# Hybrid encoder step on one core: the first branch's two early gates as a fourth Strassen pair, and two selection rounds moved

## What is computed

```python
h = rmsnorm(x, norm_mix)
(a_b, a_c, a_x, qb, kb, vb, qc, kc, vc, qi, ki, wi, g_a, g_b, g_c) = jnp.split(h @ w_in, SPLIT_POINTS, axis=-1)
y_conv, new_conv_a = causal_dwconv(a_c * a_x, conv_a_buf, conv_a)      # width 512
br_a = (a_b * y_conv) @ w_a_out                                        # 512 -> 1024
# br_b: attention in a window of 128; br_c: attention on the 256 keys that an indexer scores highest
merged = jax.nn.sigmoid(g_a) * br_a + jax.nn.sigmoid(g_b) * br_b + jax.nn.sigmoid(g_c) * br_c
x = x + merged @ w_out
```

## Time and profile before

| | |
|---|---|
| median of 3 runs | 1754.98 us (1754.83 to 1756.56) |
| profiled execution | 1755.11 us, span 1753.3 us |
| granted TensorE clock | 0.997 of full speed |
| busy, share of span | PE 98%, DVE 76%, ACT 43%, POOL 32% |
| DMA | 146.41 MB, mean 84 GB/s |

### The profile page before, as it was taken

How to read it: one execution, slowest core, us unless ns; L and a number is a source line. 1 busy time by engine, 2 the same in 40 slices (tenths; PEclk the granted TensorE clock), 3 DMA queues, 4 the chain that set the end, 5 groups by cost and what they waited for, 6 DMA issues and landing times.

```text
span 1753.3 us, 32227 instructions
## 1 busy us (share of the span) xinstructions
PE 1719.3 (98%) x12251; PEld 1679.9 (96%) x12251; DVE 1337.9 (76%) x2190; ACT 752.6 (43%) x1323; POOL 567.4 (32%) x457
## 2 busy tenths in 40 slices
PE   6999999999999999999999999999999999999998
PEld 6999999999999999888899999999999999999998
DVE  6689899868799996788759989766666665875765
ACT  5344323368721234767744563333333333422334
POOL 2211722267745431000021102655555554121030
PEclk9999999999999999999999999999999999999999
DMA  4101111111143414422324111222222222533212
GB/s 157 49 25 43 48 39 54 49 29 37 47 146 120 144 40 148 154 85 85 109 79 154 49 49 50 93 79 84 76 74 82 77 86 92 185 116 98 75 37 99
DMA packets 179189, 146.41 MB, mean 84 GB/s; under 512 B 10140, under 2 KB 149676, under 8 KB 179052
## 3 DMA queue, kind: packets, MB, share of 16 engines
q1 hardware_dynamic: 178076, 142.54, 26.2%
q0 software_dynamic: 976, 2.00, 0.5%
HBM read 118.22 MB, written 26.28 MB: 82 GB/s over the span
## 4 chain that ended last, share of the span: by engine, by line
PE 91%; DVE 4%; ACT 2%; issue 1%; POOL 1%; DMA 0%; SPq 0%; DVEq 0%; ACTq 0%; POOLq 0%
PE ps L1600 29%; PE ps L2079 23%; PE ps L2152 7%; PE ps L2138 7%; PE ps L1795 4%; PE ps L1775 4%; PE ps L1612 4%; PE ps L1712 4%; PE ps L2009 3%; PE ps L1921 3%; PE ps L1869 1%; PE ps L1630 1%; PE ps L1876 1%; ACT probs L2535 0%; DMA x_rows<-in_x_prompt 0%
## 5 line engine op out<-in xcount | busy, mean ns | idle before, releaser
L1600 PE MATMUL ps<-h_hi,w_hi 128*128 128x352 f32 (+1 forms) x768 | 168.5, 328 | 0.0
L1600 PE MATMUL ps<-h_hi,w_lo 128*128 128x352 f32 (+1 forms) x768 | 165.6, 323 | 0.0
L1600 PE MATMUL ps<-h_lo,w_hi 128*128 128x352 f32 (+1 forms) x768 | 165.2, 323 | 0.0
L1287 POOL TENSOR_TENSOR w_lo<-w_raw,w_hi 128x512 fp32r<-128x512 f32 (+1 forms) x45 | 84.9, 1886 | 236.7 <-ACT w_hi L2240 236.6
L3169 DVE MAX8 top<-key_mask 128x8 f32<-128x896 f32 (+5 forms) x166 | 151.9, 917 | 8.9 <-DVE key_mask L3169 1.4
L3169 DVE MATCH_REPLACE8 key_mask<-top,key_mask 128x896 f32<-128x896 f32 (+5 forms) x166 | 149.4, 904 | 0.0
L2079 PE MATMUL ps<-mix_hi,quarter_hi 128*128 128x264 f32 x672 | 136.9, 285 | 0.2 <-ACT x_one L2240 0.2
L2079 PE MATMUL ps<-mix_hi,quarter_lo 128*128 128x264 f32 x672 | 136.5, 285 | 0.0
L2079 PE MATMUL ps<-mix_lo,quarter_hi 128*128 128x264 f32 x672 | 136.1, 284 | 0.0
L1600 PEld LDWEIGHTS ps<-h_hi,w_lo 128*128 128x128 f32 (+1 forms) x768 | 130.7, 186 | 0.5
L1600 PEld LDWEIGHTS ps<-h_hi,w_hi 128*128 128x128 f32 (+1 forms) x768 | 128.8, 187 | 2.6 <-issue 0.9
(11 more groups left out here) (455 smaller groups left out, 4930.3 us busy)
## 6 DMA issues: line engine op xcount, KB each, us to landing
w_raw<-in_w_in SPq DMA_DIRECT2D x54, 256.0 KB, 3.1
w_hi<-gate_highs SPq DMA_DIRECT2D x48, 256.0 KB, 2.8
w_lo<-gate_lows SPq DMA_DIRECT2D x48, 256.0 KB, 3.1
ffn_tiles<-t SPq DMA_DIRECT2D x44, 264.0 KB, 2.4
w_raw<-in_w_gate SPq DMA_DIRECT2D x44, 256.0 KB, 3.1
w_raw<-in_w_up SPq DMA_DIRECT2D x44, 256.0 KB, 3.1
w_raw_in_lo<-in_w_in SPq DMA_DIRECT2D x30, 256.0 KB, 3.0
w_raw<-in_w_down SPq DMA_DIRECT2D x32, 192.0 KB, 2.7
```

The source lines that it names most:

```text
L1287: nc.gpsimd.tensor_tensor(WLO[:, k, 0:tiles, :], raw[:, k, 0:tiles, :], WHI[:, k, 0:tiles, :].bitcast(F32), ALU.subtract).then_inc(lo_read ...
L1600: last = nc.tensor.matmul(PS[0:rows, NB * k + b, 0:e - a], w[:, k, t, 0:rows], x[:, t, a:e], start=m == 0 and w is WHI and x is hi, stop=m ...
```

## The change

- `A_PAIRS` gets a fourth pair, gate tiles 0 and 1 (`C_G`, `C_G + P`). The jobs J_GA and J_GA+9 go; J_GA is now the first `w_a_out` job, and all later jobs are numbered two lower.
- The fourth pair's two tiles are t0 and t1, like the third's. ACT's first copy of it therefore waits for `a_input(2)`, which now counts on `a_added`. Even pairs now use banks 0 and 1 where odd ones use 6 and 7 (before the other way round).
- `a_conv(3)` writes to `conv_gate3` in place of t1. `a_high(2)` comes after the fourth pair's second product, `a_high(3)` after its sixth. DVE does `a_input(2)` and `a_conv(3)` before `a_lower(2)`, and the fourth pair's adds before `a_lower(3)`.
- ACT takes `Tanh` of t0 and t1 in place. DVE multiplies tile 1 by its gate in step j=2 of the `w_a_out` loop, no longer after it.
- In `attention_jobs` of the window branch the rounds of `SEL[5]` become 1, 2, 3, 3, 1 for m=1 to m=5, from 3, 2, 3, 2, 0.

```diff
-J_B = J_GA + KT + 2
+J_B = J_GA + KT
...
-A_PAIRS = (..., (C_AC + 3 * P, C_AX + 3 * P))
-A_SLOTS = [n % 4 for n in range(NQ * len(A_PAIRS) - 1)] + [2]
+A_PAIRS = (..., (C_AC + 3 * P, C_AX + 3 * P),
+           (C_G, C_G + P))
+A_GATES = 2
+A_SLOTS = [n % 4 for n in range(NQ * len(A_PAIRS))]
...
-            x = 3 if p % 2 == 0 else 0
+            x = 0 if p % 2 == 0 else 3
...
-            return 3 * p + (p == 2)
+            return 3 * p + max(p - 1, 0)
...
-        A_TILES = [(B2, B3), (T1, T3), (T0, T1)]
-        A_RAW = (T1, T0, B2, T1)
+        A_TILES = [(B2, B3), (T1, T3), (T0, T1), (T0, T1)]
+        A_RAW = (T1, T0, B2, B3)
... (PE)
-            project(J_GA, 0, 0, H_HI, H_LO)
             pe.wait_ge(a_lo, CT + 1)
-            for n in range(J_GA + 1, J_B - 1):
+            for n in range(J_GA, J_B):
                 project(0, n // 2, n % 2, A_HI, A_LO, tiles=CT)
-            project(J_B - 2, 0, 1, H_HI, H_LO)
... (ACT)
-                    act.wait_ge(*((sums_ready, 2), (taken[1], evicted(J_GA - 1)), (a_lo, 3))[p])
+                    act.wait_ge(*((sums_ready, 2), (taken[1], evicted(J_GA - 1)), (a_lo, 3),
+                                  (a_added, landed(a_adds(3))))[p])
...
-                if n == NQ * len(A_PAIRS) - 3:
-                    split(J_GA, 0, 0)
                 if n == NQ * len(A_PAIRS) - 2:
+                    split(J_GA, 0, 0, tiles=CT)
+                if n == NQ * (len(A_PAIRS) - 1) + 1:
                     a_high(2)
-            following(J_GA, 0, 0, tiles=tiles_of(J_GA + 1))
-            a_high(CT - 1)
+                if n == NQ * len(A_PAIRS) - 2:
+                    a_high(3)
+            following(J_GA, 0, 0, tiles=CT)
... (DVE)
             a_add(2, Q_A12)
-            a_lower(2)
             a_input(2)
             a_conv(3, B3)
+            a_lower(2)
+            a_add(3, Q_S4)
+            a_add(3, Q_S3)
+            a_add(3, Q_A12)
             a_lower(3)
... (DVE)
             for j in range(KT):
-                n = J_GA + 1 + j
+                n = J_GA + j
                 done(0, n // 2, n % 2)
                 if j == 0:
-                    dve.wait_ge(taken[0], evicted(J_GA))
+                    dve.wait_ge(gate_out, 1)
                     V_.scalar_tensor_tensor(tile_at(MACC, j), tokens(T0[:, 0:TOK]), 1.0, group(n % 2), ALU.add,
                                             ALU.mult).then_inc(taken[n % 2], 1)
+                if j == 2:
+                    dve.wait_ge(gate_out, A_GATES)
+                    dve.wait_ge(taken[1], evicted(J_GA + 1))
+                    V_.scalar_tensor_tensor(tile_at(MACC, 1), tokens(T1[:, 0:TOK]), 1.0, tile_at(MACC, 1), ALU.add,
+                                            ALU.mult).then_inc(a_added, 1)
                 select((SEL[5], 2))
             select((SEL[5], 2), (SEL[3], 3))
-            dve.wait_ge(gate_out, 1)
-            V_.scalar_tensor_tensor(tile_at(MACC, 1), tokens(T0[:, 0:TOK]), 1.0, tile_at(MACC, 1), ALU.add,
-                                    ALU.mult).then_inc(taken[1], 1)
-            last_low = attention_jobs(J_B, 1, R_B_V, ((NT, TOPK_S // 8), (SEL[3], 2)), ((SEL[5], 3),),
-                                      ((SEL[5], 2), (SEL[3], 1)), ((SEL[5], 3),), ((SEL[5], 2),))
+            last_low = attention_jobs(J_B, 1, R_B_V, ((NT, TOPK_S // 8), (SEL[3], 2)), ((SEL[5], 1),),
+                                      ((SEL[5], 2), (SEL[3], 1)), ((SEL[5], 3),), ((SEL[5], 3),), ((SEL[5], 1),))
```

More of the change, by code:

```diff
@@ L102 @@
 DOWN_ORDER = (Q_A11, Q_S1, Q_S2, Q_S4, Q_S3, Q_A12, Q_A22)
[L107 to L108 removed]
+A_PAIRS = ((C_AB + 2 * P, C_AB + 3 * P), (C_AC + 2 * P, C_AX + 2 * P), (C_AC + 3 * P, C_AX + 3 * P),
+           (C_G, C_G + P))
+A_GATES = 2
+A_SLOTS = [n % 4 for n in range(NQ * len(A_PAIRS))]
 A_SUMS = (Q_S1, Q_S2, Q_S4, Q_S3)
@@ L222, in tiles_of @@
 def tiles_of(n):
-    branch = J_GA < n < J_B - 1 or J_GB <= n < J_C and (n - J_GB) % 2 == 1 or J_BC <= n < J_WO
+    branch = J_GA <= n < J_B or J_GB <= n < J_C and (n - J_GB) % 2 == 1 or J_BC <= n < J_WO
     return CT if branch else KT
@@ L1078, in attention_loads @@
                         load(k, plain(k, w_in[:, :, bass.ds(i * (2 * P) + (q + k * P), P)], to=WIN))
-            load_gate_a = lambda n, j: load(n % 2, plain(n % 2, columns(w_in, C_G + j * P)))
-            free_quarters(len(A_PAIRS), 0)
-            load_gate_a(J_GA, 0)
             for j in range(KT):
-                n = J_GA + 1 + j
-                if j == 0:
-                    free_quarters(len(A_PAIRS), 1)
+                n = J_GA + j
+                if j < 2:
+                    free_quarters(len(A_PAIRS), j)
                 else:
@@ L1089, in _ @@
                 load(n % 2, plain(n % 2, columns(w_a, j * P), CT))
-            free(J_B - 2, 0, 1)
-            load_gate_a(J_B - 1, 1)
             attention_loads(J_B, C_QB, (C_KB, C_VB))
@@ L1387, in sinks @@
                     nc.gpsimd.tensor_copy(columns, pair["negative"].unsqueeze(2)).then_inc(sink_in, 1)
-            pool.wait_ge(taken[1], evicted(J_B - 1))
+            pool.wait_ge(a_added, landed(a_adds(len(A_PAIRS) - 1) + 4))
             for y in range(3):
@@ L1401, in late_gate @@
                 w, p = q // NB, q % NB
-                pool.wait_ge(gate_out, 1 + q + 1)
+                pool.wait_ge(gate_out, A_GATES + q + 1)
                 acc = piece_at(MACC, LATE_GATES[w], p)
@@ L1725, in _ @@
                 if p == 0:
+                    pe.wait_ge(taken[0], evicted(J_GA - 2))
+                elif p == 1:
                     pe.wait_ge(rows_out, R_IDX_K + 3)
-                elif p == 1:
-                    pe.wait_ge(taken[0], evicted(J_GA - 2))
                 else:
@@ L1771, in late_gates @@
                     if q >= 2:
-                        pe.wait_ge(gate_out, 1 + q - 1)
+                        pe.wait_ge(gate_out, A_GATES + q - 1)
                     for t in range(KT):
@@ L1976, in _ @@
             attend_window(WINDOW)
-            pe.wait_ge(gate_out, 1 + len(LATE_GATES) * NB)
+            pe.wait_ge(gate_out, A_GATES + len(LATE_GATES) * NB)
             gates(J_GB, O_HI, O_LO, o_lo, NT + 1)
@@ L2412, in _ @@
                     a_weight_high(n + 4)
-                if n == NQ * len(A_PAIRS) - 3:
-                    split(J_GA, 0, 0)
                 if n == NQ * len(A_PAIRS) - 2:
+                    split(J_GA, 0, 0, tiles=CT)
+                if n == NQ * (len(A_PAIRS) - 1) + 1:
                     a_high(2)
-            following(J_GA, 0, 0, tiles=tiles_of(J_GA + 1))
-            a_high(CT - 1)
[L2419 to L2423, removed]
+                if n == NQ * len(A_PAIRS) - 2:
+                    a_high(3)
+            following(J_GA, 0, 0, tiles=CT)
+            act.wait_ge(a_added, landed(a_adds(len(A_PAIRS) - 1) + 3))
+            act.wait_ge(a_copied, landed(5 * len(A_PAIRS)))
+            for gate in A_TILES[-1]:
+                nc.scalar.activation(gate[:, 0:TOK], gate[:, 0:TOK], ACT.Tanh, scale=0.5).then_inc(gate_out, 1)
+            for n in range(J_GA, J_B):
+                if n > J_GA:
+                    following(0, n // 2, n % 2, tiles=tiles_of(n + 1))
                     done(0, n // 2, n % 2)
[L2425 to L2428, removed]
+                    copy(tile_at(MACC, n - J_GA), group(n % 2)).then_inc(taken[n % 2], 1)
             def late_gate(q):
@@ L2472, in attention_jobs @@
                 if n0 == J_B:
+                    act.wait_ge(a_added, landed(a_adds(len(A_PAIRS) - 1) + 4))
                     act.wait_ge(stored[0], 32)
@@ L3298, in a_input @@
                 last = V_.tensor_tensor(U[:, SEQ + 4:TOK + 4], first[:, SEQ:TOK], second[:, SEQ:TOK], ALU.mult)
[L3299 to L3304, removed]
+                last.then_inc(a_added, 1)
+                dve.wait_ge(a_added, landed(a_adds(p + 1)))
             def a_add(p, q):
```

2 lines of the change are left out of this document (1 added, 1 removed).

## The result

The changed kernel takes **1758.58 us** (median of 22 runs, 1757.18 to 1759.75) against 1755.77 of the kernel before beside it (22 runs, 1754.6 to 1758.32): ratio 1.0016, interval 1.001 to 1.0021. It is 2.8 us slower. That is within the 0.2% which the prediction counted as no change, but above its figure of 1755.7 and outside its range, which ended at 1757.4. The forecast was built on 1754.98, the median of three runs; beside the changed kernel the median of 22 is 1755.77. So of the 2.9 us between forecast and measurement 0.8 are the base, and 2.1 are the change: +0.7 forecast, +2.8 measured. The profiled execution took 1759.71 us.

A forecast was written before the change was run, and what follows sets the result against it. PE was taken as the bound, busy 1719.3 of 1753.3 us. Terms -2.5 + 0.5 + 0.3 + 2.35 gave +0.7 on the 1754.98 us median, so 1755.7 us, range 1753.2 to 1757.4.

The forecast's parts named there:

- PE's work, -2.5: Fourth pair's 168 matmuls (20.8 us) replace two gates' 144 (23.3 us), so PE issues 2.5 us less.
- the 0.6 us of slack: In the fourth pair, ACT's first copy, waiting for `a_input(2)`, would end 0.6 us before PE wants it: cost 0.
- Entry of the `w_a` jobs, +0.5: After the fourth pair, PE waits for `a_lower(3)` and starts the `w_a` jobs at 239.2, not 238.7: +0.5 us.
- Third `w_a` job, +0.3: PE, due at 250.85, waits until 251.15 for DVE's multiply of tile 0, which has the same banks: +0.3 us.
- DVE's debt: DVE's 105.7 us of work from `a_lower(3)` on leaves it free for the value parts at 343.6, before 338.81.
- It waits 2.35 us: At J_B+4's third value-transpose group PE arrives at 342.65 and goes on at 345.0, after DVE's value low part: +2.35 us.
- Behind 359 us all is the same code ... 0: Everything after 359 us is the same code with the same partners, shifted together, so it costs 0.
- B: Rival, chance 0.17: DVE's chain is over 2 us shorter than reckoned, PE waits little and the gain stays: -1.65 us.
- C: Rival, chance 0.07: POOL work beside DVE makes `a_input(2)` and its copy late, PE stops in the fourth pair: 1756.4 to 1760.
- D: Rival, chance 0.04: the fourth pair's first weights come late, PE waits 1 to 3 us at 217.9: 1756.7 to 1758.7.

The follow-up runs named there:

- early_a3_round_m5: Changed kernel, one selection round moved from m=3 to m=5, `a_high(3)` after the fourth pair's fifth product, `a_lower(3)` before its last add: 1753.46 us (ratio 0.9989).
- v_group edits: Changed kernel with the third value-transpose group of J_B+4 after k-tile 7 or 6 in place of 5: 1754.57 us (0.9995) and 1755.53 us (1.0001).
- round_m3_to_m5: Changed kernel with one of the three selection rounds of m=3 put to m=5 (1, 2, 2, 3, 2): 1754.74 us, ratio 0.9994.
- after_look3: A further profiled execution of the changed kernel with nothing edited: 1756.34 us.

## Why the prediction was wrong

Its steps, in their order:

- **PE's work, -2.5: right**, as early_a3_round_m5 shows. The pair runs without a hole of note. `a_input(2)` took 2.34 and 1.28 us (2.28 and 1.27 forecast), and the copy ended at 222.95, where PE goes on at 222.99; the 0.6 us of slack that was forecast was not there, and in some profiles of the pair PE waits 0.2 us for this copy.
- **Entry of the `w_a` jobs, +0.5: right**, 0.47. POOL's low part ran from 235.71 for 1.30, so it lay beside the first 0.37 us of `a_lower(3)`, which took 1.48 in place of 1.26. With `a_high(3)` a product earlier the wait is gone and `a_lo` takes 1.25.
- **Third `w_a` job, +0.3: wrong**; no wait stands there. DVE began `a_lower(3)` at 236.64, with the start's 0.68 added at 237.3 and not at 237.9, and the multiply of tile 0 ended at 250.11, before PE needed its bank.
- **DVE's debt: right.** `v_parts` started at 342.72 and ended at 343.41, 342.9 to 343.6 being the forecast less the 0.68 of the start; PE went on at 344.10 (344.3), after a wait of 2.09 (2.35 forecast). Both v_group edits and round_m3_to_m5 confirm it. With the old rounds the prediction had the third group wait 5.4 us longer; the wait came before that, 5.26 us at the first matmul of J_B+4, and none was left at the third group. Body of the change where the clock does not fall: +0.51 measured, +0.7 forecast.
- **The step that failed first: "It waits 2.35 us".** The hole was priced at its own length. In three of five profiles 3.4 us behind it run at half clock and cost 1.6 us more; about 1.0 us on the mean. The earlier trace rows could not show it, having no hole in this stretch; but the range should have had a term for it. The Trainium skill (TensorE: Matmul & The Clock Gate, What's actually happening) says that the clock is set by how busy TensorE has been recently. The traces agree so far that a hole of 2.0 to 2.1 us was followed by a fall in three of five profiles, and the one of 5.3 us too.
- **The step that failed second: "Behind 359 us all is the same code ... 0".** PE's code before it was longer, and so one more block of it is fetched among the last transfers: 1.0 us in the traces. It is the larger part of the miss in executions where the clock does not fall (after_look3).

0.5 for the body, 1.0 for the clock on the mean and 1.0 to 1.1 for the fetch are 2.5 to 2.6; measured were 2.8. (The 1.0 is the tail with full clock. The 1.1 is the mean tail of the six pair profiles with 3.4 us of half clock near 1740, 5.9 us, 5.2 to 6.6, against 4.8 in three without the fetch.) Where the clock fell is known of the profiled runs alone. The mean clock of all 22 runs fits the account: the eight at 0.995 took 1759.1 us on the mean, the seven at 0.998 took 1757.7. How much of this comes from the falls near 1740 us is not shown. Why a hole of the same length brings the clock down in one execution and not in the next stays open.

Of the rivals, B's condition did not occur: DVE's chain was as long as forecast. C did not occur either, though its margin was nearly used up, and nor did D. The pair's 2.5 us were real all the time: hidden behind DVE, lost again at the output, and back as soon as both were dealt with.

## What to carry to other kernels

Before a change that makes a saturated engine's stream shorter, find the late partner that sets the next meeting point; here one round of selection (2.7 us) in a later job decides the sign. Price a hole in TensorE's stream not only at its length: the one of 2.1 us here cost 3.7 in three profiles of five. When the end of a kernel is bounded by output transfers, count the instruction fetches in the last window: a program a few instructions longer can put one there, and instructions in an idle place can move it away.

## What the runs showed of the hardware

- The granted clock fell to half for 3.4 us behind PE holes of 2.0 to 2.1 us in 3 of 5 profiles, for 6.8 us in and behind one of 5.3 us, and not behind holes of 0.5 and 1.7 us (one profile each). It also fell near 1740 us, where PE waits some 0.4 us, in 4 of 7 profiles of the kernel before and its edits and in 7 of 13 with the pair, and near 20 us, behind waits of PE of 1.7 to 3.0 us, in 9 of the 20.
- One 16 KB fetch of PE's code took 0.9 to 2.0 us (median 1.0, 20 profiles). One among the last 4.3 MB of outputs made their end 1.0 us later. The traces do not name the DMA engine of a packet; that one of the 16 was late with its share is an estimate from the last fortieths, 30 and 15 GB/s where all 16 move 410.
- DVE pays for POOL beside it nearly in full: with a POOL split of 2.38 us from the same microsecond, the two low parts of the keys took 4.71 us in place of 2.47, 2.24 more. The Trainium skill (SBUF — State Buffer, Who interferes with whom) says that such instructions exclude each other for the whole of one; this row agrees. The casts behind, free of POOL, took 1.39 in place of 3.47.
